# Eight modulation steps multiplied and added up on GpSimd instead of TensorE

## The reference, cut to what matters

```python
cond = jax.nn.silu(c)
for layer in range(2):
    mod = cond @ ada_w[layer] + ada_b[layer]          # (1024) @ (1024, 6144)
    sh_m, sc_m, gt_m, sh_f, sc_f, gt_f = jnp.split(mod, 6, axis=-1)
    h = modulate(rms_norm(x, norm_mix[layer]), sh_m, sc_m)
    mix = even_mixer(h, ...) if layer % 2 == 0 else gla_mixer(h, ...)
    x = x + gt_m[:, None, :] * mix
    h = modulate(rms_norm(x, norm_ffn[layer]), sh_f, sc_f)
    x = x + gt_f[:, None, :] * hier_moe(h, ...)
```

## Time and profile before

| | |
|---|---|
| median of 3 runs | 2400.12 us (2397.52 to 2400.67) |
| the profiled execution | 2398.54 us, of which 2396.9 us are the span of the trace |
| TensorE matmuls busy | 2109.7 us, 88% |
| VectorE, ScalarE | 620.9 us, 431.3 us |
| GpSimd | 0.2 us |
| DMA | 770.18 MB, mean 321 GB/s |
| mean granted clock | 0.99 |

### The profile page before, as it was taken

The page is one execution under the profiler, slowest core; times in us unless marked ns, Lnnn a source line. Parts: engine busy times, 40 slices in busy tenths (PEclk is TensorE's granted clock), DMA queues, the critical chain, the costliest instruction groups (busy, mean ns, idle before and its releaser), DMA issues.

```text
span 2396.9 us, 31390 instructions
## 1 busy us (share of the span) xinstructions
PE 2109.7 (88%) x13552; PEld 1328.5 (55%) x13553; DVE 620.9 (26%) x1357; ACT 431.3 (18%) x843; POOL 0.2 (0%) x4
## 2 busy tenths in 40 slices
PE   7998999676677999967767799999999899999996
PEld 4785654232233685423223378887554678885553
DVE  2654331010012223100001244314311543224212
ACT  3142111000011211100001024211211234103111
POOL 0000000000000000000000000000000000000000
PEclk8999999999999999999999999999999999999999
DMA  9339889999999537999999943219999642249996
GB/s 402 146 129 393 355 340 424 425 426 426 426 427 424 206 149 310 424 425 426 426 426 426 425 184 115 106 71 386 408 424 424 259 176 106 106 182 405 424 425 267
DMA packets 68664, 770.18 MB, mean 321 GB/s; under 512 B 7616, under 2 KB 8128, under 8 KB 10176
## 3 DMA queue, kind: packets, MB, share of 16 engines
q1 hardware_dynamic: 68256, 768.20, 77.6%
q10 hardware_dynamic: 288, 0.26, 0.1%
HBM read 767.38 MB, written 1.05 MB: 321 GB/s over the span
## 4 chain that ended last, share of the span: by engine, by line
PE 68%; DMA 28%; DVE 2%; ACT 1%; issue 0%; SPq 0%; ACTq 0%; DVEq 0%
DMA slab<-in_triples 27%; PE psum L489 17%; PE psum L521 14%; PE psum L2115 7%; PE psum L2147 7%; PE psum L786 5%; PE psum L2029 4%; PE psum L592 2%; PE psum L2043 1%; DMA slab<-in_dense 1%; PE psum L2076 1%; PE psum L1336 1%; PE psum L2055 1%; PE psum L839 1%; PE psum L2089 0%; PE psum L2083 0%
## 5 line engine op out<-in xcount | busy, mean ns | idle before, releaser
L2115 PE MATMUL psum<-slab 128*32 128x512 f32 (+1 forms) x3840 | 459.5, 599 | 217.8 <-DMA slab<-in_triples 208.0
L489 PE MATMUL psum<-slab 128*128 128x128 f32 (+4 forms) x2616 | 469.6, 337 | 5.3 <-DVE slab L1930 3.5
L489 PEld LDWEIGHTS psum<-slab 128*128 128x128 f32 (+1 forms) x2616 | 384.1, 191 | 108.7 <-issue 73.3
L2115 PEld LDWEIGHTS psum<-slab 128*32 128x32 f32 x3840 | 149.2, 110 | 523.7 <-DMA slab<-in_triples 312.6
L521 PE MATMUL psum<-slab 128*128 128x256 f32 x1504 | 339.0, 386 | 5.2 <-ACT slab L2336 2.3
L521 PEld LDWEIGHTS psum<-slab 128*128 128x128 f32 x1504 | 289.8, 193 | 52.7 <-issue 9.4
L2147 PE MATMUL psum<-slab 128*32 128x512 f32 (+1 forms) x1920 | 223.0, 596 | 0.7 <-DMA slab<-in_triples 0.7
L2186 DVE TENSOR_TENSOR slab<-psum,slab 128x512 f32<-128x512 f32 (+1 forms) x44 | 24.6, 558 | 636.7 <-PE psum L2115 486.0
L2029 PE MATMUL psum<-slab 128*128 128x256 f32 x704 | 167.9, 380 | 1.2 <-DVE slab L2190 1.2
L2029 PEld LDWEIGHTS psum<-slab 128*128 128x128 f32 x704 | 126.1, 189 | 20.9 <-issue 5.0
L2156 ACT ACTIVATE slab<-psum,slab 128x128 f32<-128x128 f32 x176 | 66.2, 456 | 316.5 <-PE psum L489 316.5
(11 more groups left out here) (436 smaller groups left out, 1397.8 us busy)
## 6 DMA issues: line engine op xcount, KB each, us to landing
slab<-in_triples SPq DMA_DIRECT2D x360, 1536.0 KB, 26.3
slab<-in_dense SPq DMA_DIRECT2D x73, 2048.0 KB, 9.9
slab<-in_pairs SPq DMA_DIRECT2D x14, 2048.0 KB, 12.0
slab<-in_pairs SPq DMA_DIRECT2D x4, 1024.0 KB, 26.7
slab<-in_dense SPq DMA_DIRECT2D x2, 1680.0 KB, 29.0
slab<-in_vec SPq DMA_DIRECT2D x1, 2589.5 KB, 32.8
slab<-in_pairs SPq DMA_DIRECT2D x8, 256.0 KB, 25.8
slab<-in_pairs SPq DMA_DIRECT2D x4, 512.0 KB, 10.4
```

What stands on the lines that cost most here:

```text
L489: ins = mm(out_ap, lhs, rhs, start=(n == 0), stop=(n == len(pairs) - 1), skip_group_check=True)
L2115: ins = mm(psum[WIN * g:WIN * g + WIN, n, :], xg[:, k, WIN * g:WIN * g + WIN], weights_of(w, j, g, extra), start=(k == 0), stop=(k == KD - ...
```

## The change

The eight later steps of layer 0 leave TensorE's hand-written order. GpSimd takes each fill as it lies in its slot: eight `tensor_scalar` multiply its eight 128 x 512 blocks, in place, by the silu(c) of their partitions; three `tensor_tensor` add 4 blocks on 4, 2 on 2, 1 on 1, the last into a buffer of its own (`mod_sum`), each after a wait for the one before. What is left is a sum over partitions. TensorE makes it for all eight in one go where the first step stood (`pe_mod_rows`: eight matmuls with ones of 32 columns), ScalarE copies two banks in one instruction, TensorE turns eight blocks, ScalarE picks the columns with two instructions. VectorE adds the bias with one instruction, without the reduction over four partial sums.

The eight fills move forward in SP's queue: `EVEN_ORDER` puts one behind each of the eight projection fills. Their slots come free by `mod_ready`, which GpSimd raises once per step. TensorE passes over these slots. The 12 steps of layer 1 stay in the inverse and scan, in groups of 2, 3, 1, 1 become 2, 2, 1, 1, and 2, 2, 1 become 1, 1, 0; the scan keeps four. Step 7 of GpSimd waits for `dots_ready` first, since its sum lies where the index queries lay. Some semaphores are merged into one (`act_copied`, `act_arg`, `act_done`) with no other effect on the order.

```diff
-        even_fills = dense_fills("even_in") + dense_fills("ada0", ADA_FIRST) + dense_fills("ada1") + dense_fills("even_out")
+        EVEN_ORDER = "ipipipipipipipip"
+        even_in, even_mod = dense_fills("even_in"), dense_fills("ada0", ADA_FIRST)
+        even_fills = dense_fills("ada1") + dense_fills("even_out")
...
+                need, need_mod = max(free[u] for u in own), max(free_mod[u] for u in own)
                 if need > at[2]:
                     sp.wait_ge(sems["unit_done"], need)
                     at[2] = need
+                if need_mod > mod_seen[0]:
+                    sp.wait_ge(sems["mod_ready"], need_mod)
+                    mod_seen[0] = need_mod
...
-                    phase(even_fills[0:1], EVEN_FREE[0:1], 0)
-                    sp.dma_start(vec[:, early:], a["vec"][:, early:]).then_inc(sems["constants_in"], 16)
-                    phase(even_fills[1:], EVEN_FREE[1:], EVEN_UNITS)
+                    ins, mods = 0, 0
+                    for kind in EVEN_ORDER:
+                        if kind == "i":
+                            fill(even_in[ins], at[1] + EVEN_IN_FREE[ins])
+                            ins += 1
+                            if ins == 1:
+                                sp.dma_start(vec[:, early:], a["vec"][:, early:]).then_inc(sems["constants_in"], 16)
+                        else:
+                            mods += 1
+                            fill(even_mod[mods - 1], 0, mods)
+                    phase(even_fills, EVEN_FREE, EVEN_UNITS)
...
+        def pool_mod(q):
+
+            q.e.wait_ge(sems["silu_c"], q.due("silu_c"))
+            for j in range(MODS):
+                w = sl(even_slot(q, "p"), KD)
+                for k in range(KD):
+                    ins = nc.gpsimd.tensor_scalar(w[:, k, :], w[:, k, :], silc[:, k:k + 1], None, ALU.mult)
+                ins.then_inc(sems["pool_step"], 1)
+                q.e.wait_ge(sems["pool_step"], q.due("pool_step"))
+                for n in (4, 2):
+                    nc.gpsimd.tensor_tensor(w[:, 0:n, :], w[:, 0:n, :], w[:, n:2 * n, :], ALU.add).then_inc(sems["pool_step"], 1)
+                    q.e.wait_ge(sems["pool_step"], q.due("pool_step"))
+                if j == 6:
+                    q.e.wait_ge(sems["dots_ready"], q.due("dots_ready", NT))
+                nc.gpsimd.tensor_tensor(mod_sum(j), w[:, 0, :], w[:, 1, :], ALU.add).then_inc(sems["mod_ready"], 1)
+
+        def pe_mod_rows(q, bank):
+            q.e.wait_ge(sems["mod_ready"], q.due("mod_ready", MODS))
+            for j in range(MODS):
+                g = j % 4
+                ins = mm(psum[32 * g:32 * g + 32, bank + j // 4, :], ones[:, 0:32], mod_sum(j), start=True, stop=True,
+                         skip_group_check=True)
+            ins.then_inc(sems["mod_rows"], 1)
...
+        def pe_mod_columns(q, bank):
+            q.e.wait_ge(sems["act_copied"], q.due("act_copied"))
+            for i in range(MODS // 4):
+                for n in range(4):
+                    ins = nc.tensor.transpose(psum[:, bank + i, P * n:P * n + P], ada_rows[:, i, P * n:P * n + P], ident)
+            ins.then_inc(sems["ada_columns"], 1)
...
             q.e.wait_ge(sems["kv_ready"], q.due("kv_ready"))
-            pe_ada(q, 1, 2)
+            pe_mod_rows(q, 2)
+            q.ada = q.ada_read = ADA
             q.e.wait_ge(sems["mats_ready"], q.due("mats_ready"))
...
-            pe_ada(q, 3, 2)
-            pe_ada_end(q)
+            pe_mod_columns(q, 2)
+            pe_mod_end(q)
             q.e.wait_ge(sems["tri_read"], q.due("tri_read"))
...
-            pe_ada(q, 3, 6)
+            pe_ada(q, 2, 6)
...
-            pe_ada(q, 2, 2)
+            pe_ada(q, 1, 2)
...
-            pe_ada(q, 2, 2)
+            pe_ada(q, 1, 2)
...
-            pe_ada(q, 1, 2)
             q.e.wait_ge(sems["tri_read"], q.due("tri_read"))
```

More of the change, by code:

```diff
@@ L339, in build @@
         ADA_FREE = [j + 1 for j in range(ADA_FIRST)]
-        EVEN_FREE = [3, 5, 7, 9, 11, 13, 15, 17] + [18 + j for j in range(2 * ADA - ADA_FIRST)] + [39, 41]
-        EVEN_UNITS = 41
+        EVEN_IN_FREE = [3, 5, 7, 9, 11, 13, 15, 17]
+        EVEN_FREE = [18 + j for j in range(ADA)] + [31, 33]
+        EVEN_UNITS = 33
         GLA_FREE = [1, 3, 5, 7, 9, 11, 13, 15, 17]
@@ L357, in _, with wait_free @@
             free = [0] * (NR * SLOT // 1024)
-            def wait_free(first, size, until):
+            free_mod, mod_seen = [0] * (NR * SLOT // 1024), [0]
+            def wait_free(first, size, until, until_mod=0):
                 own = range(first // 1024, (first + size) // 1024)
-                need = max(free[u] for u in own)
+                need, need_mod = max(free[u] for u in own), max(free_mod[u] for u in own)
                 if need > at[2]:
@@ L365, in wait_free, with fill @@
                     at[2] = need
+                if need_mod > mod_seen[0]:
+                    sp.wait_ge(sems["mod_ready"], need_mod)
+                    mod_seen[0] = need_mod
                 for u in own:
-                    free[u] = until
+                    free[u], free_mod[u] = until, until_mod
                 at[0] = (first + size) % (NR * SLOT)
-            def fill(f, until):
+            def fill(f, until, until_mod=0):
                 first = after(at[0], SLOT)
-                wait_free(first, SLOT, until)
+                wait_free(first, SLOT, until, until_mod)
                 src, n = f
@@ L470, in slot, with pass_slot, even_slot @@
             return s
+        def pass_slot(q):
+            first = after(q.at, SLOT)
+            q.at = (first + SLOT) % (NR * SLOT)
+            q.skip(f"slot{first // SLOT}", 16)
+        def even_slot(q, own):
+            while EVEN_ORDER[q.even] != own:
+                pass_slot(q)
+                q.even += 1
+            q.even += 1
+            return slot(q)
         def part(q):
@@ new lines, in pe_mod_columns, with act_mod_columns @@
+        def pe_mod_columns(q, bank):
+            q.e.wait_ge(sems["act_copied"], q.due("act_copied"))
+            for i in range(MODS // 4):
+                for n in range(4):
+                    ins = nc.tensor.transpose(psum[:, bank + i, P * n:P * n + P], ada_rows[:, i, P * n:P * n + P], ident)
+            ins.then_inc(sems["ada_columns"], 1)
+        def act_mod_columns(q, bank):
+            q.e.wait_ge(sems["ada_columns"], q.due("ada_columns"))
+            for i in range(MODS // 4):
+                ins = A.activation(mod_cols[:, 16 * i:16 * i + 16].rearrange("p (g n) -> p n g", n=4),
+                                   psum[:, bank + i, :].rearrange("p (n g r) -> p n g r", n=4, g=4)[:, :, :, 0], ACT.Copy)
+            ins.then_inc(sems["ada_read"], 1)
@@ L656, in dve_ada, with pe_mod_end, dve_mod @@
+        def pe_mod_end(q):
+            q.e.wait_ge(sems["ada_read"], q.due("ada_read"))
+        def dve_mod(q):
+            q.e.wait_ge(sems["ada_read"], q.due("ada_read"))
+            V.tensor_tensor(modc[:, 16:48], mod_cols, v("ada_b0")[:, 16:48], ALU.add).then_inc(sems["dve_step"], 1)
             q.e.wait_ge(sems["dve_step"], q.due("dve_step"))
@@ L999, in pe_even_in @@
             u.end()
+            for _ in EVEN_ORDER[q.even:]:
+                pass_slot(q)
         def act_even_in(q):
@@ L2848, in dve_sb @@
             q.e.wait_ge(sems["dve_step"], q.due("dve_step"))
-            V.scalar_tensor_tensor(out=sl_, in0=sz, scalar=-1.0, in1=sz, op0=ALU.mult, op1=ALU.max).then_inc(sems["exp_arg"], 1)
+            V.scalar_tensor_tensor(out=sl_, in0=sz, scalar=-1.0, in1=sz, op0=ALU.mult, op1=ALU.max).then_inc(sems["act_arg"], 1)
             q.e.wait_ge(sems["fox_cum"], q.due("fox_cum"))
@@ L3093, in _ @@
         def _(pool):
+            q = Engine(pool)
+            q.at, q.even = FIRST_SLOT, 0
+            for _ in range(ADA_FIRST):
+                pass_slot(q)
+            pool_mod(q)
             for l in range(2):
```

101 lines of the change are left out of this document (55 added, 46 removed).

## The result

| | before | after |
|---|---|---|
| median | 2399.14 us (2397.52 to 2400.67) | 2435.46 us (2433.76 to 2438.83) |
| profiled span | 2396.9 us | 2432.1 us |
| rotation of the index queries begins | 65.13 us | 60.44 us |
| logits begin | 112.59 us | 111.90 us |
| key products (L1389 after) begin, end | 179.98, 182.90 us | 187.35, 191.91 us |

The account below looks back on a forecast made before the run. TensorE's chain up to 282 us was taken as the bound, the rest following rigidly. 2398.5 - 10.2 = 2388.3 us for the profiled execution, which lay 1.6 us under the median, gave 2390 us; range 2386 to 2416.

Parts of the forecast that it names:

- The step of GpSimd: GpSimd's products and sums beside the projections: 13.7 us per step, bounds 9.7 and 19.5, ending at 152 us, nothing paid.
- My own rule: At TensorE's request for the sums: 17.5 us available per GpSimd step, each microsecond above costing eight.
- GpSimd is late: Rival at `pe_mod_rows`: TensorE waits 15.8 us for the sums, net +5.6, 2406 us; chance 0.15.
- I take no delay that outruns these: VectorE beside GpSimd: delays stay within slack of 6.2 us after rotary embedding and 3.9 us at the probabilities.
- The rival's estimate: VectorE and GpSimd exclude each other from keys to second convolution: 16 us on TensorE, net +6, 2406 us; chance 0.30.
- TensorE's side: Steps removed from the inverse's links and wide products: 4.3 + 2.7 + 0.5 + 2.6 + 0.1 = 10.2 us gained.
- Fills: Eight fills moved past the projections' in SP's queue cost nothing; rival that they come late: 5 us, chance 0.04.
- The rest is rigid: After TensorE's way to 282 us, the experts' fills and the rest of the program move forward by the same gain.

Follow-up runs that it names:

- the execution with fillers: The change with 90 matmuls of 256 columns, whose result nobody reads, put before TensorE's wait for GpSimd's sums: 2441.77 us in one run.
- the kernel with ScalarE's products: The change with only four steps off TensorE, their products on ScalarE and only the sums on GpSimd: 2397.14 us, ratio 0.9989 to the kernel before.
- the last one: Four steps, products on ScalarE; GpSimd's sums held back, the first ones too, until VectorE's rotations or second convolution end: 2391.52 us, ratio 0.9975 to before.

## Why the prediction was wrong

**The step of GpSimd, mis-sized.** I took 13.7 us for a step (my own terms, 8.4 and 5.5, add up to 13.9), with an upper bound of 19.5; measured were 22.2 on average, and 20.7 with nothing beside it. The sums were right: 4.53, 2.58 and 1.44 us are 8.5 us, against my 8.4. The products were not: 12.4 us undisturbed, 13.4 on average, against the 5.5 that I took from VectorE's rows. The bound failed as well, because "at worst half as fast" was a guess about the loop and nothing in the trace carried it; the products ran at 2.2 times the time taken from VectorE. The page that I cited beside it ("GPSIMD Engine Reference" of the Trainium skill) has 4497 ns for the large sum, where the trace has 4526: it agrees. Its section 4.1 calls one-input work roughly line-rate; 1.55 us for a product of 512 columns, 3.0 ns per column where the two-input sum of 2048 has 2.2, disagrees, and the measurement decides. My own rule, 17.5 us per step and eight microseconds for each one above, then gives 8 x 4.7 = 38 us; TensorE was ready for the sums at 191.9 instead of 182.8 us, which leaves 29 of it, and 29.5 were measured. The rival "GpSimd is late" had the mechanism, but at 15.8 us, and got 0.15.

**"I take no delay that outruns these" for VectorE: wrong.** Rotation to key products took 12.1 us more, the key products 1.6 more. I had granted the slack of 6.2 us at the logits and 3.9 us at the probabilities. TensorE's waits came on top of them: 3.83 us at the logits and 1.8 more for their matmuls at the lower clock, 2.3 at the probabilities (1.35 and 0.97), 1.73 at L1270 and 1.5 more at the key products, both by way of ScalarE: 11.2 of the 12.1 us. The reason I gave, that the choice of keys is made of small one-input instructions, holds for MAX8 (430 ns as before) but not for the rotary embedding, and not for `tensor_scalar`. The rival's estimate, 16 us from half a meeting each, was near the 12.1 + 1.6 = 13.7 measured, but in part by luck: it left out `tensor_scalar`, and the same program lost only 8.1 us up to the key products in the execution with fillers. That both rivals came true together I had not priced at all. VectorE's delay hides 9 us of GpSimd's lateness, since TensorE asks for the sums later, and yet both together end at +36 us, beyond my range.

**TensorE's side: right in place, 3 us too large.** 10.2 us forecast, 7.0 measured in the kernel without GpSimd's work. The first link resumed 9.34 us after the key products instead of 13.63, 4.3 us earlier as worked out. The gaps closed as forecast (10.2 us); what is missing, 3.1 us, is the granted clock behind the gaps that were left, which the sum had at nothing although I had moved cover away. In the change itself, sums to output projection took 94.49 us where 99.46 stood before, 5.0 less: the same gain, less the clock behind the long wait (1.7 us, read in the one run with the fillers).

**Fills: right.** No wait of TensorE in the stage is for a transfer, and DMA moved 211 GB/s in 80 to 100 us, in the old hole of 106.

**The rest is rigid: right.** Router to end differs by 1.7 us. Sum of the parts in the profiled execution: -4.7 (before the rotation, not the change's) + 12.1 (rotation to key products) + 1.6 (the key products) + 29.5 (wait for the sums) - 5.0 (sums to output projection) + 1.7 (router to end) = 35.2 us, which is the difference of the spans.

Open: why the convolution's 36 instructions take 588 ns in one kernel and 967 in another, and why one program loses 12.1 us in one execution and 8.1 in another. I only read that it is so. Six or eight steps placed by hand were not tried.

## What to carry to other kernels

An engine that is idle is not free: before work is given to GpSimd, ask what VectorE does at that very moment and who waits for it. Placed beside VectorE's idle stretches, with the products on ScalarE, four steps gained 0.25%; all eight on GpSimd, with no regard to VectorE, lost 1.6%. Price one instruction of each form before you multiply it by 64, and when two bounds on a path depend on the same guess, price the case in which both fail. Where a change takes TensorE's cover away, count the clock of what follows as well.

## What the runs showed that I had not expected

- A one-input `tensor_scalar` of 256 columns on VectorE waits even for a GpSimd instruction that only writes (2543 ns on average beside memsets of 2.66 us), while two-input instructions keep their 481 ns beside these.
- GpSimd multiplies 4096 columns by a broadcast operand in 7.09 us, 1.73 ns per column, and by `tensor_scalar` in eight pieces in 12.4 us, 3.0 ns per column: the form with one tensor input is the slower one. Undisturbed and at the same 512 columns it takes 1.55 us, and a sum of two inputs 1.26.
- The granted clock fell to about half after idle times as short as 2.5 us, but not every time. At one link of the inverse TensorE waited 2.45 us in several kernels: its 16 matmul records took 2.05 us in the kernel before and in the one without GpSimd's arithmetic, and 3.46 us in the last one. At the first link, after waits of about 1.6 and 0.5 us, the 32 records took 3.81 us in the kernel with ScalarE's products and 5.44 in the last one. So what a short gap costs in clock can't be read from one execution.
